# One queue for the first loads, folded biases and a second buffer for the down weights of odd experts

## The reference, cut to what matters

```
def trunk_layer(x, mod, s0_f, s0_b, n_seg, p):          # mod = silu(c) @ ada_w + ada_b
    sh1, sc1, gt1, sh2, sc2, gt2 = [mod[:, i][:, None, :] for i in range(N_MOD)]
    h = rms_norm(x, p['pre_mix_g']) * (1.0 + sc1) + sh1
    proj = h @ p['w_in']
    ...
    mix = jnp.concatenate([conv_out, rwkv_out], axis=-1) @ p['w_out']
    x = x + gt1 * rms_norm(mix, p['post_mix_g'])
    h2 = rms_norm(x, p['pre_ffn_g']) * (1.0 + sc2) + sh2
    x = x + gt2 * rms_norm(routed_ffn(h2, p), p['post_ffn_g'])

def expert_block(args):                                  # 32 experts, top 4 of each token
    idx, g, e = args
    xb = tok_pad[idx]
    gu = xb @ p['w_gu'][e] + p['b_gu'][e]
    x_glu, x_lin = gu[:, :D_FF], gu[:, D_FF:]
    ...
    act = x_glu * jax.nn.sigmoid(SWIGLU_ALPHA * x_glu) * (x_lin + 1.0)
    out = act @ p['w_down'][e] + p['b_down'][e]
    return out.astype(jnp.float32) * g[:, None]
```

## Time and profile before

| | us |
|---|---|
| median of 3 runs (lowest, highest) | 1355.5 (1353.74, 1356.8) |
| the profiled execution, its own time | 1351.76 |
| span of its instructions | 1349.7 |
| TensorE busy / VectorE / ScalarE / GpSimd | 1247.6 / 455.6 / 203.0 / 125.3 |
| HBM read, mean rate over the span | 451.23 MB, 335 GB/s |

### The profile page before, as it was taken

How to read it: one execution, slowest core, us unless ns; L and a number is a source line. 1 busy time by engine, 2 the same in 40 slices (tenths; PEclk the granted TensorE clock), 3 DMA queues, 4 the chain that set the end, 5 groups by cost and what they waited for, 6 DMA issues and landing times.

```text
span 1349.7 us, 15962 instructions
## 1 busy us (share of the span) xinstructions
PE 1247.6 (92%) x6182; PEld 595.2 (44%) x6182; DVE 455.6 (34%) x944; ACT 203.0 (15%) x398; POOL 125.3 (9%) x184
## 2 busy tenths in 40 slices
PE   0899888988979999999999999999999999999997
PEld 0587766876463333333333333333333333333333
DVE  0298988876152121321212212121321212222123
ACT  2212113322121101111010111101111010110102
POOL 1001558444000000000000000000000000000000
PEclk9899999988969999999999999999999999999999
DMA  9900462030737999999999999999999999999994
GB/s 368 359 1 1 168 252 113 14 126 9 295 125 288 424 430 429 429 428 429 428 428 430 428 429 428 428 428 429 429 428 428 429 428 429 429 428 429 429 428 169
DMA packets 42783, 452.97 MB, mean 336 GB/s; under 512 B 6160, under 2 KB 6304, under 8 KB 14944
## 3 DMA queue, kind: packets, MB, share of 16 engines
q1 hardware_dynamic: 40560, 449.66, 79.3%
q10 hardware_dynamic: 1760, 2.10, 0.5%
q0 software_dynamic: 432, 0.80, 0.3%
HBM read 451.23 MB, written 1.31 MB: 335 GB/s over the span
## 4 chain that ended last, share of the span: by engine, by line
PE 78%; DVE 12%; issue 4%; DMA 2%; ACT 2%; POOL 1%; DVEq 1%; ACTq 0%; POOLq 0%
PE bank L446 33%; PE bank L481 17%; PE bank L413 5%; PE bank L439 4%; PE bank L539 4%; PE bank L594 2%; DVE front L1119 2%; DMA front<-in_chan 2%; PE bank L729 2%; DVE front L1220 2%; PE bank L465 1%; PE bank L641 1%; PE bank L472 1%; PE bank L521 1%; ACT front L817 1%
## 5 line engine op out<-in xcount | busy, mean ns | idle before, releaser
L446 PE MATMUL bank<-ring,front 128*64 128x512 f32 x2048 | 448.4, 596 | 0.0
L446 PEld LDWEIGHTS bank<-ring,front 128*64 128x64 f32 x2048 | 144.4, 137 | 301.8 <-issue 299.7
L481 PE MATMUL bank<-ring,front 128*64 128x512 f32 x1024 | 226.8, 596 | 9.4 <-ACT front L817 9.4
L1126 DVE TENSOR_SCALAR front<-bank 128x512 f32<-128x512 f32 x32 | 22.1, 692 | 486.6 <-PE bank L446 486.6
L481 PEld LDWEIGHTS bank<-ring,front 128*64 128x64 f32 x1024 | 71.9, 137 | 143.6 <-issue 135.8
L810 ACT ACTIVATE front<-front 128x512 f32<-128x512 f32 x32 | 20.2, 631 | 490.1 <-DVE front L1126 490.1
L1148 DVE COPY front<-bank 64x512 f32<-64x512 f32 x32 | 21.9, 684 | 195.5 <-PE bank L481 195.5
L413 PE MATMUL bank<-front 128*128 128x128 f32 x544 | 66.4, 282 | 1.4 <-DVE front L1107 1.4
L413 PEld LDWEIGHTS bank<-front 128*128 128x128 f32 x544 | 64.8, 199 | 1.5 <-DVE front L1107 1.5
L423 PE MATMUL bank<-front 128*128 128x512 f32 x136 | 62.9, 605 | 0.0
L439 PE MATMUL bank<-front 32*64 32x512 f32 x256 | 61.9, 600 | 0.8 <-ACT front L803 0.8
(11 more groups left out here) (239 smaller groups left out, 1095.9 us busy)
## 6 DMA issues: line engine op xcount, KB each, us to landing
ring<-in_w_gu SPq DMA_DIRECT2D x128, 2048.0 KB, 17.3
ring<-in_w_down SPq DMA_DIRECT2D x64, 2048.0 KB, 15.7
ring<-in_ada_w SPq DMA_DIRECT2D x24, 1024.0 KB, 12.0
ring<-in_w_in SPq DMA_DIRECT2D x5, 2048.0 KB, 20.9
ring<-in_w_out SPq DMA_DIRECT2D x1, 4096.0 KB, 13.4
front<-in_x SPq DMA_DIRECT2D x2, 1024.0 KB, 6.1
front<-in_lora SPq DMA_DIRECT2D x1, 1536.0 KB, 28.8
front<-in_mod SPq DMA_DIRECT2D x2, 512.0 KB, 4.9
```

Source lines behind the costliest of these rows:

```text
L446: last = pe.matmul(ps[r][64 * hf:64 * hf + 64, :], xT[:, k, S * q:S * q + S], wgu[:, k, r * F + hf * 512:r * F + hf * 512 + 512], start=Fa ...
L481: last = pe.matmul(ps[2][64 * c:64 * c + 64, :], actT[:, m, 64 * hf:64 * hf + 64], wdn[:, k, c * 512:(c + 1) * 512], start=False, stop=(k ...
```

## The change

1. **First loads.** All go on SP's queue in the order constants, conditioning vector (now into a contiguous `condT`, and multiplied into `siluT` after), x, four slices of `ada0`, the modulation addends and gains, the other four slices, `lora1`, `chan`, the small LoRA weights, the level masks. `in_const`, `in_chan`, `in_lora` and `in_lora2` are waited for apart, each where its data is used.
2. **Modulation chain.** The addend goes in by a matmul with the identity, between the slices; one VectorE multiply is left after the last slice; the transposes become four matmuls with 8 output columns each, and the copy has 32 columns in place of 512. The first projection waits for the blocks of hT one by one.
3. **Biases.** `bgu` lies as two halves on partitions 0 to 31 and 32 to 63, so that gate and up use different rows of the array. The down bias matmuls are gone: GpSimd loads `b_down` into the first 32 rows of `outp`, the transposed gates go to `GT`, and the first `combine`, which ran on zeros, adds all of it. For this TensorE waits for the gates, transposes them and waits for `b_down` before the loop.
4. **Second down buffer.** `wdn[0]` is where it was, `wdn[1]` lies in `front`, over parts of the scans' and of the router's regions. Expert 1's down weights are loaded before the loop; in the loop down weights are loaded two experts ahead.

```diff
         def _(sp):
+            sp.dma_start(const, const_in).then_inc(s["in_const"], 16)
+            sp.dma_start(condT, cond_in).then_inc(s["in_cond"], 16)
             sp.dma_start(x0, x_in.rearrange("(g p) d -> p g d", p=P)).then_inc(s["in_x"], 16)
             for k in range(KC):
+                if k == 4:
+                    sp.dma_start(madd0, mod_in[0, :, 0:512]).then_inc(s["in_mod"], 16)
+                    sp.dma_start(mmul0, mod_in[1, :, 0:512]).then_inc(s["in_mod"], 16)
                 sp.dma_start(ada0[:, k, :], ada_w[k * P:(k + 1) * P, 0:2048]).then_inc(in_ada0[k], 16)
             sp.dma_start(lora1, lora1_in).then_inc(s["in_lora"], 16)
+            sp.dma_start(chan, chan_in).then_inc(s["in_chan"], 16)
...
             sp.wait_ge(s["st_mm"], Q)
             for hf in range(2):
-                load_dn(sp, 0, hf)
+                load_dn(sp, 0, 0, hf)
+            sp.wait_ge(s["gn_out"], Q)
+            load_dn(sp, 1, 1, 0)
             sp.wait_ge(s["mix_mm"], 2 * G)
             for b in range(2, 4):
                 load_gu(sp, 0, b)
-
-            def load_next(base, e):
+            sp.wait_ge(s["logits"], G)
+            load_dn(sp, 1, 1, 1)
...
+            def load_pairs(base):
+                with sp.Fori(0, E // 2 - 1) as i:
+                    next_gu(base + i * 2, i * 2 + 1)
+                    next_dn(base + i * 2, i * 2 + 2, 0)
+                    next_gu(base + i * 2 + 1, i * 2 + 2)
+                    next_dn(base + i * 2 + 1, i * 2 + 3, 1)
+                next_gu(base + (E - 2), E - 1)
...
                 for r in range(2):
                     for hf in range(2):
-                        pe.matmul(ps[r][64 * hf:64 * hf + 64, :], bsel[:, q, :],
-                                  bgu[:, r * F + hf * 512:r * F + hf * 512 + 512], start=True, stop=False)
+                        pe.matmul(ps[r][64 * hf:64 * hf + 64, :], bsel[E * r:E * r + E, q, :],
+                                  bgu[E * r:E * r + E, hf * 512:hf * 512 + 512], start=True, stop=False)
...
                     pe.wait_ge(s["outp_ready"], n * 4 + 6)
-                for c in range(2):
-                    pe.matmul(ps[2][64 * c:64 * c + 64, :], bsel[:, q, :], bdn[:, c * 512:(c + 1) * 512],
-                              start=True, stop=False)
-
                 pe.wait_ge(s["act_ready"], n * 2 + (q + 1))
                 pe.wait_ge(s["y_added"], n * 4 + 4)
...
                 for j in range(4):
                     last = pe.matmul(ps[0][32 * j:32 * j + 32, :], siluT[:, k, :], ada0[:, k, j * 512:(j + 1) * 512],
-                                     start=(k == 0), stop=(k == KC - 1))
+                                     start=(k == 0), stop=(k == KC - 1), skip_group_check=True)
                 last.then_inc(s["ada0_acc"], 1)
+                if k == 5:
+                    pe.wait_ge(s["madd_one"], 1)
+                    pe.matmul(ps[0], ident, madd0, start=False, stop=False, skip_group_check=True)
             pe.wait_ge(s["mod0"], 1)
             for m in range(4):
-                last = pe.transpose(ps[5][:, m * P:(m + 1) * P], mod0[:, m * P:(m + 1) * P], ident)
+                last = pe.matmul(ps[5][:, m * 8:(m + 1) * 8], mod0[:, m * P:(m + 1) * P], used_rows, start=True, stop=True)
             last.then_inc(s["mod0_tr"], 1)
...
                 if n == 0:
-                    pe.wait_ge(s["in_lora"], 96)
-                    pe.wait_ge(s["hT_a"], KC)
-                    pe.wait_ge(s["hT_v"], KC)
+                    pe.wait_ge(s["in_lora"], 16)
                     pe.wait_ge(s["modT"], 1)
...
                     for k in range(KC):
+                        if n == 0:
+                            pe.wait_ge(s["hT_a"], k + 1)
+                            pe.wait_ge(s["hT_v"], k + 1)
...
             gather(pe, 1)
+
+            pe.wait_ge(s["gate"], 2)
+            for g in range(G):
+                last = pe.transpose(ps[6][0:E, g * P:(g + 1) * P], gate[:, g, 0:E], ident)
+            last.then_inc(s["gate_tr"], 1)
+            pe.wait_ge(s["in_bdn"], 16)
             with pe.Fori(0, E // 2) as i:
                 pe_pair(pe, 0, 0, i)
...
+            a.wait_ge(s["in_cond"], 16)
+            a.activation(condS, condT, ACT.Sigmoid).then_inc(s["silu_sig"], 1)
             a.wait_ge(s["in_x"], 16)
...
-            po.dma_start(bdn, b_down).then_inc(s["in_router"], 16)
             po.wait_ge(s["y_mm"], 2 * Q)
-            po.dma_start(bgu, b_gu).then_inc(s["in_router"], 16)
+            for r in range(2):
+                po.dma_start(bgu[E * r:E * r + E, :], b_gu[:, r * F:(r + 1) * F]).then_inc(s["in_router"], 16)
+
+            po.wait_ge(s["mix_mm"], 2 * G)
+            po.memset(outp, 0.0).then_inc(s["outp_ready"], 4)
+            po.memset(GT, 0.0).then_inc(s["cleared"], 1)
+            po.wait_ge(s["outp_ready"], 4)
+            po.dma_start(outp[0:E, :], b_down).then_inc(s["in_bdn"], 16)
```

More of the change, by code:

```diff
@@ L281, in build @@
         in_ada0 = in_gu
-        in_dn = [sem(f"in_dn_{hf}") for hf in range(2)]
+        in_dn = [[sem(f"in_dn_{q}_{hf}") for hf in range(2)] for q in range(2)]
         from_block = ctx.enter_context(nc.Block())
@@ L396, in _ @@
                     sp.wait_ge(s["dn_used"], turn * (E * KC))
[L397 to L400 removed]
+                    for q in range(2):
+                        for hf in range(2):
+                            load_dn(sp, q, q, hf)
+                    load_pairs(turn * E)
             for g, out in enumerate((y_prompt, y_sample)):
```

112 lines of the change are left out of this document (58 added, 54 removed).

## The result

| | before | after |
|---|---|---|
| median of 4 runs of each in one job (lowest, highest) | 1354.62 (1347.49, 1356.8) | 1337.92 (1335.29, 1338.02) |
| the profiled execution, its own time | 1351.76 | 1337.95 |
| span of its instructions | 1349.7 | 1336.1 |

After stands to before as 0.9881, 95% interval [0.9842, 0.992]: faster. The predicted 1338 is the median of after. The gain is another matter: the kernel before gave 1350.47 (7 runs), 1350.03 (13), 1349.45 (9) and 1348.82 (9) in the four later jobs, so the three runs that the prediction started from, at 1355.5, were 5 us high. From 1350 the change is worth 12 us, and 13.6 in the spans of the two profiled executions, where 17.2 were predicted. A base that was too high and a gain that was too large cancelled: that the number came out to the microsecond is luck, and the mechanism has to be judged by its parts.

The account below looks back on a forecast made before the run. Experts bound by TensorE and transfers alike, and transfers cannot go faster. 15.4 (start) + 0.9 (first release) - 0.1 (transposes) + 1.0 (tail) = 17.2 us off 1355.5 gives 1338; forecast 1334 to 1342, range 1331 to 1347.

Parts of the forecast that it names:

- The bound: Expert loop: TensorE 57.96 us a pair, transfers 58.9; TensorE work removed there returns as waits for `wgu`.
- the lead of some four pairs: Expert loop: the transfers' head start is spent after some 4 pairs, then TensorE waits about 3.8 us a pair.
- rival A: The expert loop is TensorE's: 16 x 2.86 = 45.8 us more come off, time 1293; chance 0.03.
- The second buffer: Second down-weight buffer in the expert loop: worth 0, as the last awaited chunk stays 184th in the stream.
- The biases in the loop: Expert loop: L465 goes, 1.0 us a pair; L439 on different rows saves 1.86; nothing comes off the loop.
- The start: First loads and modulation chain: L521 starts at 33.2 instead of 48.6 us, 15.4 us earlier.
- rival B: Less gained at the start, by slower first loads or half clock through L521: 3.4 to 7.7 us less; chance 0.17.
- The first release: Start of the loop's stream: comes one L439 earlier, after expert 0's first two k; 0.9 us.
- The stream and the tail: Loop transfers stay 4.9 us a chunk; the half-pair after the last chunk loses L465, 1.0 us.
- The base: Starting time of the forecast: 1355.5 us, median of the runs, 3.7 above the profiled execution.
- D: Slower by the transfers: half of `wdn` goes to another region; 5.8 us a chunk there gives 1365; chance 0.05.
- E: Early start swallowed by an unseen load or chain before the experts; time within 0.2% of before; chance 0.03.

Follow-up runs that it names:

- 3: Changed kernel with the four bias matmuls of gate and up done twice for every expert; 1336.8 us.
- 4: Changed kernel with only half of the last gate and up chunk loaded for experts 1 to 31, all matmuls kept; 1308.03 us.
- 8: Kernel before with the change's biases alone; 1348.37 us, 0.9981 of before.
- run 1: Changed kernel with one buffer for the down weights, loaded in the order of the kernel before; 1337.03 us.
- run 6: Changed kernel with each expert's down weights issued behind its gate and up weights only from expert 9 on; 1324.6 us.
- Run 11: Changed kernel with x loaded from ScalarE's queue instead of SP's; 1330.69 us.
- run 10: Changed kernel with the channel constants and all transfers behind them issued only when `lora1` has landed; 1333.85 us.
- run 7: Changed kernel with first loads and modulation chain alone: biases as in the kernel before, one down buffer; 1338.17 us.
- run 5: Changed kernel with each expert's down weights issued behind its gate and up weights from expert 2 on; 1332.35 us.
- run 2: Changed kernel with only the last expert's gate and up weights issued ahead of its down weights; 1337.01 us.
- run 9: Changed kernel with the channel constants and all behind them issued only when the last modulation weight slice has landed; 1335.3 us.

## Why the prediction was right, and where it was not

**The bound: right.** "The experts are bound by both, to the microsecond, and the transfers cannot go faster": the pairs of after take 57.1, 55.4, 57.1, 55.7 us and from the fifth on 58.7 or 58.8, as the lead of some four pairs said, and 3, 4 and 8 show the exchange. The median chunk takes 4.892 us (4.91 predicted). TensorE's own pair was put at 55.1; it is 57.1 or 55.4, since in about every second pair the clock falls to its lower level for 3.4 us. So of the 2.86 us a pair that rival A counted on, only 1.7 would have been there, even with nothing to wait for.

**The second buffer: right**, worth 0 (run 1), by the argument given. What the prediction did not see is that it could be worth two chunks in another order (run 6).

**The biases in the loop: right.** L470 takes 1.02 us (0.93 predicted), L439 took 1.86: matmuls on different rows run at once, as the Trainium skill, TensorEngine Tiling (Array Packing), section Key Properties, says. Nothing of it came off the loop.

**The start: mechanism right, size off by 4.8 us** (10.6 in place of 15.4). The failed step is "constants and x land together at about 7.5, since in the kernel before x and the constants, the same bytes, are there at 7.4". The bytes were the same within 2%, the queues were not: with one queue x landed at 9.53 and the last slice at 32.16, where 29.0 was predicted. Run 11 showed that. (At the lower rate the sum would give 32.3 and not the 31.8 that stands there, which leaves out its own 0.6 for the state loads.) The second part is `lora1`, 5.78 us behind the last slice and not 3.7, since the small transfers share with it; run 10 showed that, and run 11 that it depends on the queues too. The start gain lies where rival B put it, 3.4 to 7.7 us less, by its first mechanism (slower first loads). At the start, B was the better forecast; that the time missed its 1342 to 1346 is owed to the base and to gains behind the start that the prediction did not have. Its second one, the half clock, cost 0.94 us: L552 took 13.69 us and not 12.75.

Three windows of after with which this is read: the time of `lora1`, then L552 at half clock and at full clock.

```profile
32.00:38.00 6.00, 2.14 (x17) 1.14 (x17) 3.47 (x10) 2.53 (x8) 0.00 (x0) 0.95 1.04 254
...
42.00:44.00 2.00, 2.00 (x6) 1.64 (x5) 0.00 (x0) 0.00 (x0) 0.00 (x0) 0.50 1.03 386
44.00:48.00 4.00, 4.00 (x19) 3.47 (x19) 0.00 (x0) 1.67 (x2) 1.68 (x1) 0.98 1.05 386
```

In the first, the rate is 254 GB/s beside a DMA share of 1.04: the engines are occupied, but move less. The clock, 0.50 from 38 us on, is back at its upper level at 44, 6 us after L552's start.

**Between the start and the loop: not predicted.** 2.2 us more come off between L558 and the first L470. The scans vary by up to 5 us between profiles, so this is no effect of the change that could be shown.

**The first release: 0.9 predicted, 2.5 measured.** The step counted L439's halving (0.84 us) and not the clock. Before, the first matmuls of L446 fell on a dip; the windows of before (first) and after (second) on them:

```profile
407.90:413.40 5.50, 5.50 (x20) 1.69 (x20) 0.00 (x0) 0.00 (x0) 0.00 (x0) 0.69 0.01 3
```

```profile
395.20:399.00 3.80, 3.80 (x22) 1.33 (x20) 0.00 (x0) 0.38 (x1) 0.00 (x0) 1.00 0.02 4
```

5.45 us at a mean granted clock of 0.69 (0.50 for the first 3.4 us) became 3.86 at 1.00. It comes with part 3 of the change: with the loads alone (run 7) these matmuls begin at 0.50 again, with the biases alone (run 8) at 1.00. The shorter L470 is not needed for it, since in run 3, with the bias matmuls done twice, the clock is 1.00 too. The new transposes in front of these matmuls are the nearest thing left; that it is they was not tried.

**The stream and the tail.** The stream was predicted unchanged. It is 1.86 us longer: three times in each profile a chunk lands late behind the one before it, in all by 4.29 us over the median (2.59 before), the largest at 429.0, where a chunk came 7.28 us after the one before it. The tail is 1.1 us shorter, 1.0 predicted. So the sum runs 14.36 - 1.86 + 1.1 = 13.6 us, the difference of the spans.

**The base.** The prediction took 1355.5, the median of three runs, though the profiled execution of 1351.76 stood 3.7 below it. Over all jobs the kernel before ran between 1347.2 and 1356.8, and its time goes with its mean granted clock: at 0.983 or 0.984 it is 1347.2 to 1350.5, at 0.981 or 0.982 it is 1350.1 to 1354.9, at 0.980 it is 1354.3 to 1356.4. Only one of its executions was profiled, so which stage has the lower clock in the slower ones is not known. From a base of 1350 the same sum would have given 1333, and the measured 1338 would have been 5 above it. None of the rivals A, D and E showed.

## What to carry to other kernels

When two resources are within a microsecond of each other, as here, look at the delay from issue to landing over the whole loop: if it grows, the transfers are the bound, even where the chain that ended last names only TensorE, and work taken from TensorE comes back as waits. The second buffer gave nothing by itself; it was worth what the order of issue did with it, and that had to begin neither so early that the queue ran dry (run 5) nor so late that TensorE could not use the lead (run 2). Take the base of a forecast from more runs than three, and when a rate is taken over from the kernel before, ask whether as many queues issue it. Compare two variants stage by stage, and not by the whole time alone: of the 13.3 us between run 6 and after, 3.8 are not the order's.

## What the runs showed of the hardware

- **One queue did not fill the DMA engines at the start, two did**: 275 against 418 to 420 GB/s from 4 to 8 us. In the loop, with 2 MiB transfers, the one queue of SP gives 428.
- **Transfers on one queue overlap.** `lora1` (1.5 MiB) landed 3.66 us after its predecessor when nothing was behind it and 5.78 with small transfers behind it, but 3.95 with them when x was on the other queue (run 11); a small transfer issued behind it can land before it (run 9, one of the small LoRA weights at 36.38, `lora1` at 37.70).
- **Matmuls on disjoint rows and columns of the array run at once in float32**: the eight records of the gate and up biases take 1.02 us (L470), and took 1.86 when they shared 32 rows (L439).
- **In the loop the clock fell only behind one wait of 1.9 us.** In every pair TensorE stands once, in front of the transposes, for VectorE: 1.9 us in the twelve kernels without the down bias matmuls, 0.9 us in before and in run 7, which have them. In the twelve, 6 to 8 of the 16 pairs have a stretch of 3.4 us at the lower level (0.50), each beginning within 2 us behind that wait; before and run 7 have none. The 32 records of L508 then take 8.71 us, and 7.09 at full clock, and the pair 57.1 us in place of 55.4. The waits of the matmuls for `wgu`, 1.3 us at most, had no such stretch behind them. That the wait is the cause is argued from this and was not tried by itself, and why only some of the pairs have it is open. The wait in before and in after (total us, times, longest), the lower level in after, and the 6 us behind it:

```profile
PE bank L472 <- DVE front L1119: 13.9, 16, 0.9
PE bank L499 <- DVE front L1160: 30.1, 16, 1.9
699.60:702.80 3.20, 3.14 (x8) 1.03 (x10) 0.55 (x4) 0.20 (x1) 0.00 (x0) 0.50 1.01 430
703.00:709.00 6.00, 6.00 (x34) 1.78 (x30) 0.59 (x1) 0.59 (x1) 0.00 (x0) 1.00 1.02 434
```
